# Expert steps with the quarter unit's gate and up products first, down products in turns, and bodies in the order 64, 160, 96, 256

## The reference

```python
def _swiglu(h, wg, wu, wd):
    return (jax.nn.silu(h @ wg) * (h @ wu)) @ wd

logits = h @ w_router
top_val, top_idx = lax.top_k(logits, TOP_K_EXPERTS)      # 2 of 8 for each token
gate = jax.nn.softmax(top_val, axis=-1)
...                                                       # the tokens of each expert are gathered
def expert_block(args):
    xb, e = args
    return _swiglu(xb, w_gate[e], w_up[e], w_down[e])     # 1024 -> 3584 -> 1024
...
return jnp.zeros_like(h).at[tok_s].add(y_assign)          # weighted sum back to the tokens
```

## Time and profile before

| | us |
|---|---|
| median of 3 runs (1689.62 to 1693.55) | 1691.92 |
| profiled execution, its own time | 1689.38 |
| its span in the trace | 1687.6 |
| PE busy, share of the span | 92% |
| experts, first to last product | 695 to 1673 |

### The profile page before, as it was taken

How to read it: one execution, slowest core, us unless ns; L and a number is a source line. 1 busy time by engine, 2 the same in 40 slices (tenths; PEclk the granted TensorE clock), 3 DMA queues, 4 the chain that set the end, 5 groups by cost and what they waited for, 6 DMA issues and landing times.

```text
span 1687.6 us, 20427 instructions
## 1 busy us (share of the span) xinstructions
PE 1550.0 (92%) x8346; PEld 834.1 (49%) x8347; DVE 416.8 (25%) x892; ACT 253.0 (15%) x501; POOL 0.2 (0%) x4
## 2 busy tenths in 40 slices
PE   5988899999999988896999999899998999988996
PEld 3777668777567874532444433233332333332332
DVE  1366535333245442501000020010110200201004
ACT  2132310000023231111100111110111111111111
POOL 0000000000000000000000000000000000000000
PEclk9999899999999988898999999999999999999998
DMA  9974525665765530499455679999999999999992
GB/s 348 379 256 170 179 100 212 250 249 199 281 223 189 181 119 13 173 407 405 187 199 206 253 285 400 408 407 361 379 408 407 407 396 357 406 408 407 389 383 97
DMA packets 168182, 484.41 MB, mean 287 GB/s; under 512 B 10024, under 2 KB 20544, under 8 KB 168000
## 3 DMA queue, kind: packets, MB, share of 16 engines
q1 hardware_dynamic: 168128, 483.68, 75.5%
HBM read 482.61 MB, written 1.05 MB: 287 GB/s over the span
## 4 chain that ended last, share of the span: by engine, by line
PE 78%; SPq 7%; DVE 5%; DMA 5%; ACT 2%; issue 2%; ACTq 0%; DVEq 0%
PE bank L944 14%; PE bank L998 12%; PE bank L878 9%; PE bank L725 8%; PE bank L955 6%; PE bank L940 6%; SPq L592 5%; PE bank L896 4%; PE bank L859 3%; DMA ring<-in_w_exp_up 3%; PE bank L992 3%; PE bank L719 2%; PE bank L1083 2%; DMA ring<-in_w_exp_down 1%; SPq L598 1%
## 5 line engine op out<-in xcount | busy, mean ns | idle before, releaser
L944 PE MATMUL bank<-ring,hT 128*64 128x448 f32 x1792 | 348.9, 542 | 13.7 <-DMA ring<-in_w_exp_up 9.3
L998 PE MATMUL bank<-ring,bt 128*32 128x256 f32 (+1 forms) x1680 | 237.2, 493 | 13.1 <-ACT bt L1725 11.3
L944 PEld LDWEIGHTS bank<-ring,hT 128*64 128x64 f32 x1792 | 124.3, 137 | 230.2 <-issue 189.4
L1525 DVE TENSOR_TENSOR bt<-arena,bank 128x512 f32<-128x512 f32 (+2 forms) x52 | 35.3, 679 | 793.5 <-PE bank L944 523.7
L878 PE MATMUL bank<-hT,ring 128*128 128x256 f32 x704 | 157.4, 384 | 1.4 <-DVE hT L1218 1.4
L998 PEld LDWEIGHTS bank<-ring,bt 128*32 128x32 f32 (+1 forms) x1680 | 81.8, 124 | 150.6 <-issue 114.8
L725 PE MATMUL bank<-hT,ring 128*128 128x256 f32 x640 | 152.6, 396 | 3.7 <-ACT hT L1612 2.5
L878 PEld LDWEIGHTS bank<-hT,ring 128*128 128x128 f32 x704 | 134.9, 192 | 23.8 <-issue 3.8
L725 PEld LDWEIGHTS bank<-hT,ring 128*128 128x128 f32 x640 | 124.2, 198 | 25.6 <-DVE hT L1218 4.2
L1137 DVE SCALAR_TENSOR_TENSOR acc<-ring,cond,acc 128x512 f32<-128x512 f32 x140 | 105.2, 752 | 4.9
L955 PE MATMUL bank<-ring,hT 128*32 128x448 f32 x1024 | 102.8, 542 | 0.0
(11 more groups left out here) (245 smaller groups left out, 1007.3 us busy)
## 6 DMA issues: line engine op xcount, KB each, us to landing
ring<-in_w_exp_gate SPq DMA_DIRECT2D x128, 896.0 KB, 8.5
ring<-in_w_exp_up SPq DMA_DIRECT2D x128, 896.0 KB, 13.8
ring<-in_w_exp_down SPq DMA_DIRECT2D x64, 1536.0 KB, 13.9
ring<-in_w_ada SPq DMA_DIRECT2D x24, 2048.0 KB, 9.4
ring<-in_w_in SPq DMA_DIRECT2D x10, 2048.0 KB, 12.9
ring<-in_w_exp_down SPq DMA_DIRECT2D x32, 512.0 KB, 15.2
ring<-in_w_ff_gate SPq DMA_DIRECT2D x5, 2048.0 KB, 12.4
ring<-in_w_ff_up SPq DMA_DIRECT2D x5, 2048.0 KB, 12.8
```

The lines of the kernel that those rows point to most:

```text
L944: last = mm(o[64 * c2:64 * c2 + 64, 64 * c2:64 * c2 + EH], xsT[:, k, t0:t0 + 64], w[:, k, c2 * EH:(c2 + 1) * EH], start=(k == 0), stop=(k ...
L998: last = mm(bank[4 + 2 * u][m * c:m * c + m, 0:D // parts], hsT[:, u, at_:at_ + m], ed[:, t, c * (D // parts):(c + 1) * (D // parts)], sta ...
```

## The change

- `UNITS` puts the quarter first. In a step of the 96 and 160 bodies the quarter's gate and up products come first (waiting for a piece of gate and a piece of up together), then the gate and up products of the half or wide unit, with the quarter's transposition after two chunks of the up products.
- The half or wide unit is now the last item, so it is the one that gives pieces of gate and up up; it now does this in its own gate and up products.
- The down products of both units take turns: three tiles of the quarter, the transposition of the last item, two more of the quarter, three of the half or wide unit, and so on. The 256 body also takes turns.
- Halves and quarters are turned by four transpositions (before two transpositions and four small products), and ACT copies them in three pieces (before in one).
- `scatter` writes banks 3, 5, 6 and 7, and waits for both copies first. Sums of the quarter move to bank 4, of the other unit to 6 and 7.
- The bodies follow each other in the order 64, 160, 96, 256.

```diff
-UNITS = {1: [("half", 0)], 2: [("half", 0), ("quarter", 64)], 3: [("wide", 0), ("quarter", 128)],
+UNITS = {1: [("half", 0)], 2: [("quarter", 64), ("half", 0)], 3: [("quarter", 128), ("wide", 0)],
          4: [("wide", 0), ("wide", 128)]}
...
-            def quarter(t0, ks):
-
-                for k in ks:
+            def quarter(J, n, t0):
+
+                for k in range(KC):
+                    if k % 2 == 0:
+                        pe.wait_ge(full_g[k // 2], 16 * J + 16)
+                        pe.wait_ge(full_u[k // 2], 16 * J + 16)
...
-                        if k % 2 and q % 2:
-                            last.then_inc(u_used if q == 3 else g_used, 1)
+                        if k == KC - 1 and q % 2:
+                            last.then_inc((eg_p, eu_p)[q // 2], before_last(n, 0))
...
-                    for t in (1, 2):
-                        nc.tensor.transpose(o[:, t * m:(t + 1) * m], h[:, t * P:(t + 1) * P], one_)
-                    mm(o[:, 0:m // 2], h[:, 0:P], one_[:, 0:m // 2], start=True, stop=True)
-                    mm(o[:, 3 * m:3 * m + m // 2], h[:, 3 * P:4 * P], one_[:, m // 2:m], start=True, stop=True)
-                    for c2 in range(2):
-                        last = mm(o[64 * c2:64 * c2 + 64, m // 2:m], h[:, 64:P] if c2 else h[:, 3 * P:EH],
-                                  one_[:, c2 * m // 2:(c2 + 1) * m // 2], start=True, stop=True)
+                    for t in range(4):
+                        last = nc.tensor.transpose(o[:, t * m:(t + 1) * m], h[:, t * P:(t + 1) * P], one_)
...
                 elif n == 2:
-                    hidden(r, J, n, 0, 0, A)
-                    hidden(r, J, n, 0, 1, A)
+                    quarter(J, n, A[1])
+                    hidden(r, J, n, 1, 0, B)
                     pe.wait_ge(yzero_v, r + 1)
-                    quarter(B[1], range(0, 6))
-                    turn_hidden(J, n, 0, "half", bank[3])
-                    quarter(B[1], range(6, KC))
-                    down(J, n, 0, range(0, 4), (0,))
-                    pe.wait_ge(eh_v, 4 * J + done(n, 1))
-                    down(J, n, 0, range(4, 5), ())
-                    turn_hidden(J, n, 1, "quarter", bank[7])
-                    down(J, n, 0, range(5, ET), ())
-                    down(J, n, 1, ALL, (1,))
+                    pe.wait_ge(eh_v, 4 * J + done(n, 0))
+                    hidden(r, J, n, 1, 1, B, 0, range(0, 2))
+                    turn_hidden(J, n, 0, "quarter", bank[3])
+                    hidden(r, J, n, 1, 1, B, 0, range(2, KC))
+                    down(J, n, 0, range(0, 3), (0,))
+                    turn_hidden(J, n, 1, "half", bank[7])
+                    down(J, n, 0, range(3, 5), ())
+                    down(J, n, 1, range(0, 3), (1,))
+                    down(J, n, 0, range(5, 6), ())
+                    down(J, n, 1, range(3, 6), ())
+                    down(J, n, 0, range(6, 7), ())
+                    down(J, n, 1, range(6, 7), ())
...
             def scatter(r, n):
...
+                pe.wait_ge(ys_a, r + 1)
+                pe.wait_ge(ys_v, r + 1)
                 for hf in range(2):
-                    pe.wait_ge((ys_a, ys_v)[hf], r + 1)
...
-                    with pe.If(which == 2):
-                        expert(r, 2)
+                    with pe.If(which == 3):
+                        expert(r, 3)
                     with pe.Else():
-                        with pe.If(which == 3):
-                            expert(r, 3)
+                        with pe.If(which == 2):
+                            expert(r, 2)
...
-                    m = 7 * (64 if kind == "half" else 32)
-                    ins = act(hsT[:, u, 0:m], o[:, 0:m], ACT.Copy)
+                    m = 64 if kind == "half" else 32
+                    act(hsT[64:P, u, 8 * m:9 * m], o[64:P, m:2 * m], ACT.Copy)
+                    act(hsT[0:64, u, 8 * m:9 * m], o[0:64, 6 * m:7 * m], ACT.Copy)
+                    ins = act(hsT[:, u, 0:8 * m], o[:, 0:8 * m], ACT.Copy)
```

More of the change, by code:

```diff
@@ L249 @@
 CAPS = (64, 96, 160)
-UNITS = {1: [("half", 0)], 2: [("half", 0), ("quarter", 64)], 3: [("wide", 0), ("quarter", 128)],
+UNITS = {1: [("half", 0)], 2: [("quarter", 64), ("half", 0)], 3: [("quarter", 128), ("wide", 0)],
          4: [("wide", 0), ("wide", 128)]}
-TURNED_AT = (0, 2, 4, 3, 5, 6, 1)
+TURNED_AT = (0, 2, 4, 3, 5, 7, 8)
 ITEMS = {n: sum(2 if kind == "wide" else 1 for kind, _ in units) for n, units in UNITS.items()}
@@ L928, in _, with hidden @@
                         last.then_inc(gat_p, 1)
-            def hidden(r, J, n, i, a, unit, c=0):
+            def hidden(r, J, n, i, a, unit, c=0, ks=range(KC)):
                 kind, t0 = unit
                 w, o, last_item = (eg, eu)[a], bank[a], i == ITEMS[n] - 1
-                for k in range(KC):
+                for k in ks:
                     if i == 0 and k % 2 == 0:
                         pe.wait_ge((full_g, full_u)[a][k // 2], 16 * J + 16)
-                    if i == 0 and a == 1 and k == 0:
+                    if i == (1 if n in (2, 3) else 0) and a == 1 and k == 0:
                         pe.wait_ge(sgt_a, r + 1)
@@ L1029, in step @@
+                    turn_hidden(J, n, 1, "half", bank[7])
[5 more added lines that the diff above has]
+                    down(J, n, 1, range(6, 7), ())
                 elif n == 3:
-                    hidden(r, J, n, 0, 0, A, 0)
-                    hidden(r, J, n, 0, 1, A, 0)
@@ L1032, in step @@
-                    pe.wait_ge(esg_a, 4 * J + done(n, 0))
-                    hidden(r, J, n, 1, 0, A, 1)
+                    quarter(J, n, A[1])
+                    hidden(r, J, n, 1, 0, B, 0)
                     pe.wait_ge(yzero_v, r + 1)
[L1035 to L1045, removed]
+                    pe.wait_ge(eh_v, 4 * J + done(n, 0))
+                    hidden(r, J, n, 1, 1, B, 0, range(0, 2))
+                    turn_hidden(J, n, 0, "quarter", bank[3])
@@ new lines, in step @@
+                    hidden(r, J, n, 1, 1, B, 0, range(2, KC))
+                    pe.wait_ge(esg_a, 4 * J + done(n, 1))
+                    hidden(r, J, n, 2, 0, B, 1)
+                    pe.wait_ge(et_a, 4 * J + done(n, 0))
+                    turn_hidden(J, n, 1, "wide", bank[3], 0)
+                    hidden(r, J, n, 2, 1, B, 1)
+                    down(J, n, 0, range(0, 3), (0,))
+                    turn_hidden(J, n, 2, "wide", bank[5], 1)
+                    down(J, n, 0, range(3, 5), ())
@@ L1046, in step @@
+                    down(J, n, 1, range(0, 3), (1, 2))
+                    down(J, n, 0, range(5, 6), ())
+                    down(J, n, 1, range(3, 6), ())
+                    down(J, n, 0, range(6, 7), ())
+                    down(J, n, 1, range(6, 7), ())
                 else:
@@ L1062, in step @@
                     hidden(r, J, n, 3, 1, B, 1)
-                    down(J, n, 0, ALL, (0, 1))
+                    down(J, n, 0, range(0, 3), (0, 1))
                     turn_hidden(J, n, 3, "wide", bank[3], 1)
-                    down(J, n, 1, ALL, (2, 3))
+                    down(J, n, 0, range(3, 4), ())
+                    down(J, n, 1, range(0, 3), (2, 3))
+                    down(J, n, 0, range(4, 6), ())
+                    down(J, n, 1, range(3, 6), ())
+                    down(J, n, 0, range(6, 7), ())
+                    down(J, n, 1, range(6, 7), ())
             def scatter_matrix(r, n):
@@ L1078, in scatter @@
                 tiles = range(2 if n > 2 else 1)
+                pe.wait_ge(ys_a, r + 1)
+                pe.wait_ge(ys_v, r + 1)
                 for hf in range(2):
-                    pe.wait_ge((ys_a, ys_v)[hf], r + 1)
                     for b in range(2):
                         for q in tiles:
-                            last = mm(bank[(2, 6)[hf] + b][:, :], selgT[:, q, b * P:(b + 1) * P],
+                            last = mm(bank[((3, 5), (6, 7))[hf][b]][:, :], selgT[:, q, b * P:(b + 1) * P],
                                       ys[:, q, hf * CW:(hf + 1) * CW], start=(q == 0), stop=(q == tiles[-1]))
@@ L1532, in expert_end @@
                 ve.wait_ge(d_used, 3 * ES * r + 3 * ES)
+                first_ = bank[4 if n in (1, 4) else 6]
                 if n < 3:
-                    last = nc.vector.tensor_copy(ys[0:64, 0, CW:D], bank[4][64:P, :])
+                    last = nc.vector.tensor_copy(ys[0:64, 0, CW:D], first_[64:P, :])
                 else:
-                    last = nc.vector.tensor_copy(ys[:, 0, CW:D], bank[5][:, :])
+                    last = nc.vector.tensor_copy(ys[:, 0, CW:D], bank[5 if n == 4 else 7][:, :])
                 if n in (2, 3):
@@ L1540, in expert_end @@
                         last = nc.vector.tensor_copy(ys[s0:s0 + 32, q, c * T:(c + 1) * T],
-                                                     bank[6][32 * c:32 * c + 32, 0:T])
+                                                     bank[4][32 * c:32 * c + 32, 0:T])
                 elif n == 4:
@@ L1564, in _ @@
```

(19 more changed lines are left out.)

## The result

| | before | after |
|---|---|---|
| median of 6 runs each, us | 1692.74 (1689.34 to 1694.04) | 1699.26 (1696.86 to 1702.59) |
| ratio, 95% interval | | 1.0046 (1.0034 to 1.0059) |
| profiled execution, its span, us | 1687.6 | 1700.8 |

What follows compares the result with a forecast made beforehand. 64 steps wait for loads, others for PE; the queue binds the 96/64 cycle, then PE. Terms -4.8 + 6.8 + 5.8 = +7.8 us on the 1691.9 median give 1699.7; range 1690 to 1713.

Steps and rivals of the forecast that it cites:

- Up to the queue's restart at the 64 expert: From entry into the 160 body until the queue restarts at 1008: -5.5, +0.5 for three steps, +0.2 expert end, -4.8 us.
- the "issue" piece ahead of the 160 body: PE's 10.48 us idle gap at the branch from the 64 to the 160 body, taken as gone; first step ends 5.5 earlier.
- The rival that the piece stays, at 10.5: Gap stays at the 160 body as a first-visit cost; 0.7 us won instead of 5.5, total 1704.5; chance 0.15.
- Length of steps: One step of PE: 96 body 30.0 us (+0.1), 160 body 48.92 us (+0.16).
- the term for transpositions: In a 96 step, four transpositions each: quarter's 0.52 us (-0.40), half's value 0.80 us (-0.23).
- the 0.17 us wait for ACT's three copies: In a 96 step, the half's down products wait for ACT's copies: +0.17 us, bounds 0 and 0.3.
- Entry into the 96 body: From landing of the last up piece to the next step, PE needs 25.49 us instead of 19.43, +6.1.
- Landing cycle: Cycle of a 96 and a 64 expert between landings of the last up piece: 226.4 us, +3.4, twice.
- a gap that moves to the 96 body: Rival: the issue gap comes at entries of the 96 body, 4 to 5 us each, 13 at three, 1713; chance 0.08.
- PE's way: The 96/64 cycle followed through PE's work, boundary and next landing: 220.3 us before, 226.9 after, then binding instead of the queue's.
- Last expert: From its up landing to the end, 109.9 us before, 25.5 + 90.0 after: +5.6, with the boundary +5.8.
- PE has 2.7 us to spare: In the kernel before, the queue's way binds the 96/64 cycle by 2.7 us: 223.0 against PE's 220.3.

Runs made afterwards that it cites:

- the run with the later wait: Changed kernel with gate products of the half or wide unit first, then quarter, then up, and PE's wait for the quarter's hidden values behind three up chunks: 0.9935, 1680.69 us.
- The two additions to the kernel before: Kernel before with down products in turns alone: 1.0020; kernel before with four more transpositions of the half's hidden values in each 96 step: 1.0022.
- the changed kernel with extra work: Changed kernel with four more transpositions of the half's hidden values in each 96 step: ratio to the kernel before 1.0070 (1.0057 to 1.0083).

## Why the prediction was right, point by point

- **The total.** Forecast +7.8 us, 1699.7; measured +7.8 us by the ratio, a median of 1699.26. That the two agree so closely is in part luck. Up to the end of the last scatter the two profiled executions differ by 8.8 us: -4.5 up to the restart, -0.9 from there to the first landing (a term that the forecast doesn't have), +8.0 and +1.4 for the two cycles, +4.8 for the last expert. An unforeseen "issue" piece added about what the shorter steps took off.
- **Up to the queue's restart at the 64 expert: -4.8 forecast, -4.5 measured** (1006.39 less 699.59 against 1006.44 less 695.16). Inside it, I took the "issue" piece ahead of the 160 body as gone. It was 4.11 us (4.1 to 4.4 in every kernel with the new order). It lay almost wholly under the loads; what it cost was the slow clock behind it, 1.7 us in the quarter's products (7.82 instead of 6.15). So -3.6 us came instead of -5.5; at the full clock it would have been -5.3. The sum had no term for such a clock. The 1.42 us on the way back, which I had kept, are gone in all six kernels with the changed step. The rival that the piece stays, at 10.5, fell as well.
- **Length of steps.** 160 step 48.92 forecast, 48.89 measured. 96 step 30.0 forecast, 29.57 measured: the term for transpositions was too cautious (0.39 us for the quarter's four where I had 0.52, 0.59 for the half's where I had 0.80), and the 0.17 us wait for ACT's three copies did not come (1127.73 + 1.00 us of down products, next at 1128.75), because ACT's third copy starts (1128.12) while the second still runs (to 1128.22). Ends of stretches cost what the earlier trace rows gave, 0.14 to 0.17 us.
- **Entry into the 96 body: 25.49 us forecast, 25.14 measured,** where the kernel before needs 19.43. This is the cause, and it is shown: with the gate products under the loads again, and steps as long as in the changed kernel, 19.13 us pass and the ratio goes from 1.0046 to 0.9935.
- **Landing cycle: +3.4 each forecast.** The undisturbed one came to +1.4 (224.86 against some 223.5), for the shorter steps: 25.14 + 88.72 + 5.66 (boundary) + 1.82 + 103.52 = 224.86. That is PE's way, the mechanism that was forecast; its size was 226.4. The first came to +8.0. What I had put in a rival, a gap that moves to the 96 body, came at another place: not on the way into it, but on the first way back, 3.79 us and 2.6 us of slow clock. I had argued that the ways back show no gap; that held for the old places of the bodies only. The Trainium skill's rule (Runtime: NRT & Kernel Launch, Instruction fetch mechanics), that a taken branch out of the window waits for a fetch, goes with the piece coming and going with the body's place in three pairs of kernels that differ in that alone. The traces bear it out in part only: by that rule the second way back, the same branch, would wait as the first does, and it shows no piece in any kernel. The entry into the 96 body behind the 160 body's code shows none either where it could be seen: in the run with the later wait, products start right behind the last of the boundary (1096.52 + 0.38 us, then 1096.83).
- **Last expert: +5.8 forecast, +4.8 measured** (1558.71 to 1673.20 before, 1567.10 to 1686.42 after), again for shorter steps.
- **A statement that was wrong without harm:** that today's cycle is bound by the queue and PE has 2.7 us to spare. The two additions to the kernel before show that most of a longer step is paid, because PE's steps stand in the queue's way too. The formula for it (25.5 + 60.0 + 7.7, then 129.7) held those steps; the sentence about slack did not.
- **The signs.** Seen: PE idle from the scatter to the first up piece (4.25 us), the DMA share running out as 64 experts begin, the lengths of entry and steps. Not seen: the 160 body without an "issue" piece ahead of it.

## What to carry to other kernels

With single buffers and loads that alternate with PE as the bound, look at what PE can do while the last piece to arrive is still on its way: work that needs only the pieces that have come must stand before work that needs both. An earlier release of buffers buys nothing by itself where the next bound is PE's rest after the landing: here the load-only way was 222.0 us in a cycle of 224.9. It pays once that rest is short again (218.2). When a product is moved, count also what it hid, here the 1.5 us of silu and product behind the quarter.

## What was not expected of the hardware

The time that PE stands under "issue" at a branch depends on where the body lies. With the 160 body behind the 96 body it is 10.2 to 10.5 us in five kernels, directly behind the 64 body 4.1 to 4.4 us in five, and the first way back from the 96 body costs 2.2 to 4.1 us when that one lies third and nothing when it lies second. At later visits of the same bodies it is nothing. Between 785 and 802 us, with the 10.48 us piece, the DMA view of the kernel before lists these fetches of instructions (queue, kind: packets, MB, share):

```profile
q8 instruction: 3, 0.05, 1.2%
```

The changed kernel has two in each of its stretches with a piece, 785 to 802 (4.11 us) and 1222 to 1240 (3.79 us):

```profile
q8 instruction: 2, 0.03, 0.8%
```

The kernel before has none in 1218 to 1240, where no piece stands. But the changed kernel also has two packets in 1000 to 1010, where PE doesn't wait. That these fetches are what PE waits for was not shown; it is the reading that fits most of the rows.

After such idle time the granted clock can be below full. It was at half (0.50) in 1234 to 1240 in the changed kernel, which cost 2.6 us beside the piece's own 3.79, and 0.72 in 1228 to 1234 in the kernel before with the new order (13.50 us instead of 12.20). A wait for loads can do it too: in the changed kernel with extra work it was 0.50 in 1560 to 1563, after 4.23 us of waiting for the first piece of up, and the quarter's products took 8.98 us instead of 6.15.
